# Two-layer encoder trunk on one core: four moves in the order of work, and norms 1 and 3 by halves of the tokens

## What is computed

```python
cond = jax.nn.silu(c)
for l in range(DEPTH):
    mod = cond @ ada_w[l] + ada_b[l]
    sh1, sc1, g1, sh2, sc2, g2 = jnp.split(mod, 6, axis=-1)
    h = modulate(rms_norm(x, norm_mix_g[l]), sh1, sc1)
    y = stick_window_mixer(...) if l % 2 == 0 else hgrn2_mixer(...)
    x = x + g1[:, None, :] * y
    h = modulate(rms_norm(x, norm_ffn_g[l]), sh2, sc2)
    x = x + g2[:, None, :] * conv_ffn(h, ...)
return rms_norm(x, final_g)
```

## Time and profile before

| | us |
|---|---|
| median of 3 runs | 1359.72 (1358.35 to 1359.87) |
| the profiled execution, its own time | 1360.04 |
| its span, first to last instruction | 1358.2 |
| PE busy | 1323.5 (97%) |
| DVE busy | 808.7 (60%) |
| ACT busy | 558.1 (41%) |
| mean granted TensorE clock | 0.993 |

### The profile page before, as it was taken

How to read it: one execution, slowest core, us unless ns; L and a number is a source line. 1 busy time by engine, 2 the same in 40 slices (tenths; PEclk the granted TensorE clock), 3 DMA queues, 4 the chain that set the end, 5 groups by cost and what they waited for, 6 DMA issues and landing times.

```text
span 1358.2 us, 17432 instructions
## 1 busy us (share of the span) xinstructions
PE 1323.5 (97%) x6281; PEld 1083.0 (80%) x6281; DVE 808.7 (60%) x1197; ACT 558.1 (41%) x837; POOL 46.9 (3%) x92
## 2 busy tenths in 40 slices
PE   6999998899999999999999999999999999999998
PEld 5877776777888888888778888888788888888786
DVE  5745557567666656436697777775765455552423
ACT  6656554334333333212255555553343333332212
POOL 1000000000000000001100000000000000000000
PEclk9999999999999999999999999999999999999998
DMA  9543431153544555465622222224523333332232
GB/s 336 167 124 109 125 109 32 46 164 103 150 142 143 150 146 147 141 184 190 210 82 78 76 65 63 74 67 125 155 78 95 105 93 93 94 107 93 82 100 81
DMA packets 190148, 160.38 MB, mean 118 GB/s; under 512 B 5271, under 2 KB 163176, under 8 KB 190098
## 3 DMA queue, kind: packets, MB, share of 16 engines
q1 hardware_dynamic: 177696, 116.34, 28.5%
q0 software_dynamic: 11856, 42.68, 10.4%
q10 hardware_dynamic: 546, 0.69, 0.1%
HBM read 157.59 MB, written 2.10 MB: 118 GB/s over the span
## 4 chain that ended last, share of the span: by engine, by line
PE 89%; DVE 5%; ACT 2%; SPq 1%; issue 1%; DMA 1%; DVEq 0%; ACTq 0%
PE proj L1603 61%; PE z L1603 22%; PE obank L1603 3%; PE misc L1603 2%; SPq L479 1%; DVE ada_sum L1118 1%; DMA w_raw<-ab_w_in 1%; DVE normed L1056 0%; ACT w_hi L621 0%; DVE hT_lo L1062 0%; SPq L489 0%; DVE soft L1220 0%; ACT q_sb L741 0%; DVE w_lo L1018 0%; DVE xT L1410 0%
## 5 line engine op out<-in xcount | busy, mean ns | idle before, releaser
L1603 PE MATMUL proj<-hT_hi,w_hi 128*128 128x512 f32 x1112 | 441.5, 397 | 4.6 <-DVE hT_lo L1062 4.1
L1603 PE MATMUL proj<-hT_hi,w_lo 128*128 128x512 f32 x1112 | 433.7, 390 | 0.0
L1603 PE MATMUL proj<-hT_lo,w_hi 128*128 128x512 f32 x1112 | 433.4, 390 | 0.0
L1018 DVE TENSOR_TENSOR w_lo<-w_raw,w_hi 128x1024 fp32r<-128x1024 f32 x189 | 231.2, 1224 | 338.6 <-ACT w_hi L621 338.6
L621 ACT ACTIVATE w_hi<-w_raw 128x1024 fp32r<-128x1024 f32 x191 | 202.0, 1059 | 442.7 <-PE proj L1603 261.2
L1603 PEld LDWEIGHTS proj<-hT_hi,w_hi 128*128 128x128 f32 x1112 | 209.2, 188 | 57.2 <-DVE hT_lo L1062 8.0
L1603 PEld LDWEIGHTS proj<-hT_hi,w_lo 128*128 128x128 f32 x1112 | 209.0, 188 | 44.4
L1603 PEld LDWEIGHTS proj<-hT_lo,w_hi 128*128 128x128 f32 x1112 | 209.3, 188 | 43.3 <-issue 1.7
L1603 PE MATMUL z<-gated_hi,w_hi 128*128 (+1 forms) x264 | 104.5, 396 | 0.2 <-DVE xT L1410 0.2
L1603 PE MATMUL z<-gated_hi,w_lo 128*128 (+1 forms) x264 | 102.8, 389 | 0.0
L1603 PE MATMUL z<-gated_lo,w_hi 128*128 (+1 forms) x264 | 102.8, 389 | 0.0
(11 more groups left out here) (326 smaller groups left out, 1620.6 us busy)
## 6 DMA issues: line engine op xcount, KB each, us to landing
ada_raw<-ada_w POOLq DMA_DIRECT2D x80, 512.0 KB, 4.3
w_raw<-ffn_w_gate SPq DMA_DIRECT2D x44, 512.0 KB, 3.8
w_raw<-ffn_w_up SPq DMA_DIRECT2D x44, 512.0 KB, 3.9
w_raw<-ffn_w_down SPq DMA_DIRECT2D x44, 512.0 KB, 3.4
w_raw<-hg_w_in SPq DMA_DIRECT2D x32, 512.0 KB, 4.1
ada_first<-ada_w SPq DMA_DIRECT2D x16, 512.0 KB, 10.9
w_raw<-ab_w_in SPq DMA_DIRECT2D x14, 512.0 KB, 5.0
w_raw<-ab_w_out SPq DMA_DIRECT2D x8, 512.0 KB, 4.4
```

Of the source, the lines that this page charges most:

```text
L1018: nc.vector.tensor_tensor(w_lo[:, slot, :], w_raw[:, slot, :], w_hi[:, slot, :].bitcast(F32), ALU.subtract).then_inc(lo_done, 1)
L1603: return nc.tensor.matmul(dst, weights_ap, moving, start=start, stop=stop, skip_group_check=True)
```

## The change

Seven places, none of which changes a weight, a layout or a large product.

1. Opening, PE: the four `keep_clock` matmuls ahead of `quad(1)` and the wait for `x_new` go; two of the same kind stand ahead of the wait for the second half of `first_used`.
2. Window heads, DVE: `window_copy(0)` moves ahead of `window_max(2)` and of a weight split.
3. Last window head, PE: the first two chunks of the output projection's unit pair move ahead of `window_values(6)`, with waits for head 6's copies before them (the pair writes the banks from which those copies read).
4. Last projection, PE and ACT: the final transposes of the first half and ACT's copy move from before the loop over the second half's units to behind it.
5. ACT, norms 1 and 3: the split of unit u0+9 moves ahead of the last square.
6. Norms 1 and 3: the last residual, the last square, the sum by ones, Ln, Exp, and chunk 0's `normed`, `hT_hi` and `hT_lo` are done in two halves of 256 tokens. The second half's sum goes to bank z0.
7. DVE, norms 1 and 3: the order becomes normed 0 (two halves), low 0 (two halves), normed 1, normed 2, low 1.

```diff
@@ scalar: new for norms 1 and 3
+            def last_square(n):
+                act.wait_ge(ss_done, 5 * n)
+                act.wait_ge(x_first, n // 2 + 1)
+                nc.scalar.activation(square[:, 1, token_halves[0]], xT[:, DC - 1, token_halves[0]], ACT.Square
+                                     ).then_inc(sq_first, 1)
+                act.wait_ge(x_new, 8 * n + DC)
+                nc.scalar.activation(square[:, 1, token_halves[1]], xT[:, DC - 1, token_halves[1]], ACT.Square
+                                     ).then_inc(sq_done, 1)
+            def root_halves(n):
+                first, second = token_halves
+                act.wait_ge(misc_full, MISC_AT[f"norm{n}"] + 1)
+                nc.scalar.activation(rstd[:, first], misc[:, first], ACT.Ln, bias=EPS, scale=1.0 / D).then_inc(misc_free, 1)
+                act.wait_ge(misc_free, MISC_AT[f"norm{n}"] + 1)
+                nc.scalar.activation(rstd[:, first], rstd[:, first], ACT.Exp, scale=-0.5).then_inc(rstd_first, 1)
+                act.wait_ge(sum_second, n // 2 + 1)
+                nc.scalar.activation(rstd[:, second], zb[0][:, second], ACT.Ln, bias=EPS, scale=1.0 / D
+                                     ).then_inc(log_second, 1)
...
@@ scalar: out_units (norms 1 and 3)
-                    elif o < DC - 1:
+                    else:
                         split(u0 + o + 2, o % 2)
-                    squares(n, o)
-                split(u0 + DC + 1, 1)
-                root(n)
+                    if o < DC - 1:
+                        squares(n, o)
+                last_square(n)
+                root_halves(n)
                 modulated(n)
@@ scalar: down
                 split(u0 + HALF + 2, 1)
+                with act.Fori(0, HALF // 2 - 1) as i:
+                    for s in range(2):
+                        split(u0 + HALF + 3 + 2 * i + s, s)
                 if last:
                     act.wait_ge(misc_full, MISC_AT["fin"] + 1)
                     nc.scalar.activation(out_nat[:, TB - 1, 0:512], misc[:], ACT.Copy).then_inc(misc_free, 1)
-                with act.Fori(0, HALF // 2 - 1) as i:
-                    for s in range(2):
-                        split(u0 + HALF + 3 + 2 * i + s, s)
@@ vector: normalise, chunk 0 by halves where n is odd
+                    for i, half in enumerate(token_halves):
...
+                            dve.wait_ge(rstd_first, n // 2 + 1)
+                        else:
+                            dve.wait_ge(rstd_done, n)
+                        nc.vector.scalar_tensor_tensor(out=normed[:, 0, to], in0=xT[:, 0, half],
+                                                       scalar=scale_g[:, n, 0:1], in1=rstd[:, half],
...
+                    for i, half in enumerate(token_halves):
...
+                        low_half = nc.vector.scalar_tensor_tensor(
+                            out=hT_lo[:, 0, half], in0=normed[:, 0, to], scalar=shift[:, 0:1],
+                            in1=hT_hi[:, 0, half].bitcast(F32), op0=ALU.add, op1=ALU.subtract)
+                    low_half.then_inc(h_lo, 1)
-                for dc in range(DC + 1):
+                for dc in range(n % 2, DC + 1):
@@ vector: window heads
             window_norm(1)
+            window_copy(0)
             window_max(2)
             split(U_OUT0 + 1, 1)
-            window_copy(0)
@@ vector: out_units
-                    nc.vector.scalar_tensor_tensor(out=xT[:, o, :], in0=out_banks[o % 4][:],
-                                                   scalar=mod[:, gate, o:o + 1], in1=xT[:, o, :],
-                                                   op0=ALU.mult, op1=ALU.add).then_inc(x_new, 1)
+                    for half in token_halves if o == DC - 1 else [slice(0, SEQ)]:
+                        last = nc.vector.scalar_tensor_tensor(out=xT[:, o, half], in0=out_banks[o % 4][:, half],
+                                                              scalar=mod[:, gate, o:o + 1], in1=xT[:, o, half],
+                                                              op0=ALU.mult, op1=ALU.add)
+                        last.then_inc(x_new if half.stop == SEQ else x_first, 1)
@@ tensor: norm_sum
-                mm(misc[:], ones, sumsq[:], start=True)
-                for s in range(2):
-                    pe.wait_ge(sq_done, 8 * (n - 1) + 7 + s)
-                    last = mm(misc[:], ones, square[:, s, :], stop=(s == 1))
-                last.then_inc(misc_full, 1)
+                if n % 2:
+                    first, second = token_halves
+                    mm(misc[:, first], ones, sumsq[:, first], start=True)
+                    mm(zb[0][:, second], ones, sumsq[:, second], start=True)
+                    pe.wait_ge(sq_done, 8 * (n - 1) + 7)
+                    mm(misc[:, first], ones, square[:, 0, first])
+                    pe.wait_ge(sq_first, n // 2 + 1)
+                    mm(misc[:, first], ones, square[:, 1, first], stop=True).then_inc(misc_full, 1)
+                    mm(zb[0][:, second], ones, square[:, 0, second])
+                    pe.wait_ge(sq_done, 8 * n)
+                    mm(zb[0][:, second], ones, square[:, 1, second], stop=True).then_inc(sum_second, 1)
...
@@ tensor: opening
             x_columns(range(3, 6))
+            misc_wait("first1")
+            keep_clock(misc, 2)
             pe.wait_ge(first_used, 2 * DC)
-            misc_wait("first1")
             first_sums(1)
             x_columns(range(6, DC))
-            pe.wait_ge(x_new, 6)
-            keep_clock(zb[3], 4)
@@ tensor: last window head
+                    pe.wait_ge(pt_act, h)
+                    pe.wait_ge(pt_dve, h)
+                    unit_pair(U_OUT0, h_base["o0"], range(0, 2))
                     window_values(h - 1)
-                    unit_pair(U_OUT0, h_base["o0"], range(0, 2))
                     window_transposes(h)
@@ tensor: down
                 one(u0 + HALF, 1, 0, first=True, mod_group=(8, None)[layer], banks=down_banks[1])
+                with pe.Fori(0, HALF // 2 - 1) as i:
+                    for s in range(2):
+                        one(u0 + HALF + 1 + 2 * i + s, s, 4 * i + 2 * s + 2, banks=down_banks[1])
                 if layer:
                     pe.wait_ge(fin_y, 4)
...
                     final_transposes(0, range(TB - 1, TB), range(4)).then_inc(misc_full, 1)
-                with pe.Fori(0, HALF // 2 - 1) as i:
-                    for s in range(2):
-                        one(u0 + HALF + 1 + 2 * i + s, s, 4 * i + 2 * s + 2, banks=down_banks[1])
                 last_two(u0 + FB - 2, 0, FB - 4, down_banks[1])
```

41 lines of the change are left out of this document (38 added, 3 removed).

## The result

The changed kernel takes 1352.32 us in the median of 5 runs (1350.67 to 1353.21); the kernel before takes 1359.72 (5 runs, 1358.35 to 1361.47). The ratio is 0.9946, 95% interval 0.9932 to 0.9960: 7.4 us less, where 8.1 were forecast (1351.6). The profiled execution is the fastest of the five: 1350.67 us, span 1348.7, granted clock 0.999.

What follows compares the result with a forecast made beforehand. The prediction took PE, busy 97% of the span, as the bound, with gains only in its waits, half clock and unread matmuls. Terms 1.0 + 2.3 + 3.4 + 1.5 - 0.1 = 8.1 us less: 1351.6 us, range 1349.8 to 1354.6.

Steps and rivals of the forecast that it cites:

- Opening: Ahead of quad(1): low matmuls start sooner, 1.0 us gained if the clock still falls; ends 0.5 and 2.0.
- rival (a): Opening: the clock stays up as the new matmuls fill the only gap ahead of the fall; 1350.6 us, chance 0.2.
- passes through whole: From quad(1) to the window heads: no PE waits there, so the opening's gain arrives undiminished.
- First heads: First window heads: earlier copy of head 0 removes DVE's idle time for late logits, net 2.3 us; ends 0 and 2.9.
- Rival (b): First window heads: gain not passed on, something other than late logits sets the round; 1353.9 us, chance 0.12.
- Last head: Last window head: unit pair fills PE's wait for the obank copy, 3.4 us gained; ends 1.9 and 3.5.
- rival (c): Last window head: the clock falls under the unit pair again; 1353.1 us, chance 0.08.
- Final transposes: Last projection: 1.5 of PE's 2.05 us wait go, 0.5 stay for w_lo; ends 1.0 and 2.05.
- Norms: Norms 1 and 3: the halves' gain is taken back, 0.1 us lost together; ends 1.4 lost and 0.8 gained.
- the three reasons: Norms 1 and 3: split ahead of the square (0.55 us), dearer halves (0.17 us a step), PE free no sooner.
- Rival (d): Norms 1 and 3: halves bring PE's first block and low 1 forward by 0.4 us each; 1350.8 us, chance 0.1.
- Rival (e): Whole kernel slower: clock falls on dense work, 1.5 us each; seven give 1362.1 us, chance 0.02.

Runs made afterwards that it cites:

- e6: The kernel before with only the unit pair moved ahead of head 6's values; one execution, 1357.04 us.
- e9: The changed kernel with the opening's change (part 1) undone; median 1354.11 us, ratio 0.9952.
- e3: The kernel before plus the opening's change alone; median 1361.16 us, ratio 1.0006.
- e5: The kernel before with only the move of window_copy(0); one execution, 1358.76 us.
- e8: The changed kernel with DVE making normed 1 ahead of low 0 behind norms 1 and 3; one execution, 1350.34 us.
- e7: The changed kernel with the split of unit u0+9 back behind the last square in norms 1 and 3; one execution, 1350.87 us.
- e12: e10 plus two unread matmuls in the recurrence's head 0, none added in the opening; median 1350.41 us, ratio 0.9928.
- e10: The changed kernel with the edits of e7 and e8 together; median 1351.91 us, ratio 0.9938.
- e11: e10 plus unread matmuls at three places: two ahead of the first 128x1 sums, two ahead of quad(0), two in the recurrence; median 1351.56 us, ratio 0.9937.

## Why the prediction was right, and where it was not

- **Sum and median.** 8.1 us forecast, 9.4 in the profiled execution (1360.04 to 1350.67), 7.4 in the median. The median lies inside the range, 0.7 us from the forecast. Of the 9.4 us, 0.68 were there before the change is reached; the four moves came to 1.68 (opening) + 5.75 (both at the heads) + 1.52 (final transposes) = 8.95, where 8.2 were forecast. The profiled execution of the change is one without any fall of the clock in the work; the others, 1.3 to 2.5 us longer, were not profiled, and that they have falls is likely but not shown. That the median came so close is therefore partly luck: the opening's term was too small by 0.7, and the median gained less than the profile. The prediction read the falls of one profile as a property of the kernel. For the two behind the long waits at the heads that holds in every profile, for the opening and the recurrence it doesn't.
- **Opening.** Forecast 1.0 with the clock falling, 2.0 without. Measured 1.68 and 1.86 in rows, with the clock at 1.00: rival (a), which had a chance of 0.2. My argument against it, that the row of 128x1 sums stays as sparse as it was, was wrong: it does stay sparse, and yet in none of the eight profiles that have the new opening does the clock fall there. (It fell at `quad(0)`, at 25 to 31 us, in four of them instead. Of the six profiles with the old opening, e6 fell at `quad(0)` alone, e9 at both places, and the other four, the kernel before's among them, at 42 to 47 us alone.) e6 also shows what the gain is made of. It is the old opening without the fall at 42 to 47 us:

```profile
41.47 1.84 PE L1603 MATMUL misc<-table,ada_sum 128*128 128x1 f32 x16
...
45.93 0.39 PE L1603 MATMUL z<-hT_lo,quad_w 128*128 128x512 f32 x1
```

  From the sums to the first low matmul that is 4.46 us, 6.19 in the kernel before and 4.47 in the changed one (4.18 to 4.29 in the other seven with the new opening). So nearly all of the opening's 1.7 us is the fall, and the moved matmuls by themselves are worth 0.3 us at most. The 1.0 us that the prediction gave the order at half clock could not be seen, as no profile with the new opening fell there; at full clock `quad(1)` waits for ACT's `hT_hi` instead (0.53 us in the change). Which of the two edits spares the fall, the matmuls added or the four taken away, was not tested.
  By the rule of the Trainium skill (TensorE: Matmul & The Clock Gate, "HAM oscillation — how this bites in real kernels") the clock should have had no reason to fall; that sets the size right for the changed kernel, but the reason that it names, long idle gaps, doesn't describe the falls in the opening and in the recurrence, ahead of which no wait is longer than 0.74 us. That the gain "passes through whole" to the window heads holds, in e3 too: its heads' interval is 205.07 us, 205.19 before.
- **First heads.** Forecast 2.3, measured 2.45 (e5). Rival (b) is out. The size was right, the account left a part out: the prediction named half clock in the opening and at the end of the heads only, and took DVE's 2.9 us for late logits without saying that PE had made them at half clock, from 213.6 us on.
- **Last head.** Forecast 3.4, measured 3.28 (e6), at full clock: rival (c) is out. PE's gap was 1.61 us, as forecast (1.6). The spared fall is some 1.4 us of it: the pair and head 6's values together took PE 6.06 us before (246.35 to 252.41) and take 4.63 (239.67 to 244.30).
- **Final transposes.** Forecast 1.5 with 0.5 left as a wait for `w_lo`; measured 1.52, with 0.59 left. That their new place costs nothing shows in the same stretch, which holds both places: it is 1.52 us shorter, and the wait shrank by 1.46 (2.05 to 0.59).
- **Norms.** Forecast 0.1 us lost, measured 0.06 gained in norm 1 and 0.09 lost in norm 3 (the third chunk at 9.18 before, 9.27 after). The size was right, of the three reasons one: DVE's order (e8). The split cost 0.1 us and not 0.55, since ahead of the Ln it costs the same (e7). The third, that PE is free no sooner, was half right: chunk 0's block did start 0.61 us sooner, straight behind the unread matmuls and with no wait ahead of it, and only that chunk 1 is what counts made it worthless. That halves are dear on ACT (0.38 and 0.42 us a step where 512 columns took 0.60 and 0.63) is seen, but their overlap pays for it, so that the lower end of 1.4 us lost was far off: in e8 chunk 1 stands 0.42 us nearer to the last residual than before in norm 1 (7.46 and 7.88) and 0.28 in norm 3 (7.45 and 7.73). Rival (d) would have been nearly right with the old order: 0.7 us in both norms together, where it had 0.8.
- **Rival (e)** was the right thing to fear with the wrong count: falls do turn up on dense work (1.4 to 1.5 us each at 695 to 705 us), with the old opening as often as with the new, yet no profile had more than three in the work, as before.

## What to carry to other kernels

Read a pipelined stage behind a norm at the second chunk, not at the first: splitting the first chunk to start early is worth nothing if it puts the second chunk's work behind it. When an edit's row shows a gain, list the stretches at half clock of both profiles and ask how much of the gain is the clock: of the 9.5 us here some 4.7 are three spared falls, by my estimate from rows (1.7 in the opening, 1.6 at the first heads, 1.4 at the last), and only the two behind long waits came and went with the code in every profile. Filling a short wait behind a row of sparse matmuls with matmuls whose result nobody reads may pay: with two of them at one place the median was 1.5 us lower here (e12 and e10, not clear of noise), while with four more in the opening, in waits that they nearly fill, it was 1.15 us higher (e11).

The lowest median is e12's: 1350.41 us, 1.9 below the change. It beats the kernel before; against the change it is not clear of noise, as the intervals of the two ratios overlap. e1, the four moves without the halves, has 1350.89 us and is the simpler program.

## What the runs showed of the hardware that I had not expected

The granted clock fell to 0.50 where PE had hardly stood still. In the recurrence the wait ahead of it is 0.48 us (e1, e3, e5, e6, e9, e10), at `quad(0)` it fell in or just behind a wait of 0.67 to 0.74 us (e1, e6, e12), and in e8, e9 and e10 it fell at 25.5 to 26.4 us, ahead of any wait there longer than 0.15 us and up to 0.8 us behind the end of the 128x1 row (25.5 us in e8). A wait of 2.05 us with 128x512 matmuls ahead and 128x128 transposes behind did not bring it down. What the falls in the opening and the recurrence share is a row of sixteen 128x1 matmuls shortly ahead. In the recurrence no fall was seen with the short wait filled (e11, e12), but six of the twelve profiles with the wait unfilled had none either, so it wasn't shown that the wait is needed. The same row and the same wait go with a fall in one profile and without one in another. e1's executions lie in two clusters 2.3 us apart; the profiled one, in the upper cluster, has two falls, and none of the lower was profiled. That is more than the opening's term or the final transposes'.
